# Gated delta rule: two heads to a step on a common beat, the inverse built from 32x32 blocks

## What is computed

```python
g = jnp.cumsum(g, axis=-1)                                  # per chunk
decay = jnp.exp(where(causal, g[c] - g[s], -inf))
lower = where(strict, (k_beta @ k.T) * decay, 0)
t_inv = inverse(eye + lower)                                # unit lower triangular
u = t_inv @ v_beta;  w = t_inv @ (k_beta * eg)
qk = where(causal, (q @ k.T) * decay, 0)
# over the chunks, state S:
v_new = u - w @ S;  o = q_g @ S + qk @ v_new;  S = S * exp(g_last) + k_dec.T @ v_new
o = rms_norm(o, gdn_norm_w) * silu(z)
```

## Time and profile before

| | us |
|---|---|
| median of 3 runs | 921.08 (913.3, 921.08, 924.0) |
| the profiled execution | 913.96 |
| its span, first to last instruction | 912.2 |
| PE busy in the span | 881.9 |
| DVE busy | 669.5 |
| ACT busy | 508.0 |
| POOL busy | 72.1 |

### The profile page before, as it was taken

One profiled execution on the slowest core, in us unless ns is written; L12 is line 12 of the kernel. 1 busy time (PEld: TensorE's weight loads), 2 busy tenths in 40 slices (PEclk: granted clock), 3 DMA queues, 4 the chain that ended last, 5 costly groups with the idle time before them and its releaser, 6 DMA issues.

```text
span 912.2 us, 18654 instructions
## 1 busy us (share of the span) xinstructions
PE 881.9 (97%) x8020; PEld 840.6 (92%) x8020; DVE 669.5 (73%) x1132; ACT 508.0 (56%) x822; POOL 72.1 (8%) x91
## 2 busy tenths in 40 slices
PE   5897999999999999999999999999999999999997
PEld 2797899999898989999999999999888999999997
DVE  3877877566979687677888885578666778888653
ACT  2489668453344637655354444556665567666442
POOL 0101122021001101020000000220000200000011
PEclk9999999999999999999999999999999999999999
DMA  8754232332776664465998889635332436555631
GB/s 337 277 190 170 93 137 97 139 139 97 248 259 230 233 231 164 167 216 182 269 338 292 286 291 259 227 121 189 137 141 93 182 139 210 207 185 175 251 130 47
DMA packets 27681, 177.31 MB, mean 194 GB/s; under 512 B 2864, under 2 KB 5680, under 8 KB 7504
## 3 DMA queue, kind: packets, MB, share of 16 engines
q1 hardware_dynamic: 27600, 176.13, 55.1%
HBM read 174.29 MB, written 1.84 MB: 193 GB/s over the span
## 4 chain that ended last, share of the span: by engine, by line
PE 76%; DVE 10%; ACT 7%; DMA 4%; issue 1%; POOL 1%; DVEq 0%; SPq 0%; ACTq 0%
PE ps L1094 42%; PE ps L1100 20%; DVE wl L1851 3%; DMA raw<-in_w_fi_dram 2%; ACT wh L1459 2%; DVE acc L1750 2%; PE ps L1092 2%; PE ps L1139 1%; PE ps L1147 1%; PE ps L1233 1%; PE ps L1150 1%; PE ps L1098 1%; DMA raw<-in_ada_dram 1%; DMA raw<-in_w_sc_dram 1%; DVE KT L1733 1%
## 5 line engine op out<-in xcount | busy, mean ns | idle before, releaser
L1851 DVE TENSOR_TENSOR wl<-raw,wh 128x1024 fp32r<-128x1024 f32 x265 | 322.0, 1235 | 76.2 <-ACT wh L1459 75.5
L1094 PE MATMUL ps<-HH,wh 128*128 128x256 f32 x1480 | 367.4, 285 | 0.7 <-ACT HH L1433 0.2
L1094 PE MATMUL ps<-HH,wl 128*128 128x256 f32 x1480 | 357.4, 278 | 0.0
L1459 ACT ACTIVATE wh<-raw 128x1024 fp32r<-128x1024 f32 x265 | 273.4, 1042 | 140.3 <-PE ps L1100 109.2
L1094 PEld LDWEIGHTS ps<-HH,wh 128*128 128x128 f32 x1480 | 279.2, 189 | 8.2 <-issue 2.9
L1094 PEld LDWEIGHTS ps<-HH,wl 128*128 128x128 f32 x1480 | 278.9, 188 | 0.4
L1100 PE MATMUL ps<-HL,wh 128*128 128x256 f32 x1480 | 226.6, 278 | 0.3 <-DVE HL L1796 0.3
L1100 PEld LDWEIGHTS ps<-HL,wh 128*128 128x128 f32 x1480 | 195.2, 188 | 0.6 <-DVE HL L1796 0.5
L1094 PE MATMUL ps<-FH,wh 128*128 128x256 f32 x352 | 84.5, 276 | 0.0
L1094 PE MATMUL ps<-FH,wl 128*128 128x256 f32 x352 | 84.5, 276 | 0.0
L1750 DVE SCALAR_TENSOR_TENSOR acc<-raw,silc,acc 128x512 f32<-128x512 f32 x101 | 76.3, 756 | 8.0 <-DMA raw<-in_ada_dram 5.0
(11 more groups left out here) (273 smaller groups left out, 1088.2 us busy)
## 6 DMA issues: line engine op xcount, KB each, us to landing
raw<-in_ada_dram SPq DMA_DIRECT2D x32, 1024.0 KB, 5.4
raw<-in_w_fi_dram SPq DMA_DIRECT2D x22, 1024.0 KB, 5.0
raw<-in_w_up_dram SPq DMA_DIRECT2D x22, 1024.0 KB, 4.8
raw<-in_w_rest_dram SPq DMA_DIRECT2D x20, 1024.0 KB, 4.7
raw<-in_w_in_dram SPq DMA_DIRECT2D x16, 1024.0 KB, 4.8
raw<-in_w_qkv_dram SPq DMA_DIRECT2D x12, 1024.0 KB, 4.8
raw<-in_w_o_dram SPq DMA_DIRECT2D x8, 1024.0 KB, 4.9
raw<-in_w_fo_dram SPq DMA_DIRECT2D x8, 1024.0 KB, 4.9
```

The costliest lines, as they stand in the source:

```text
L1094: e.matmul(o, w[:, k, 128 * t:128 * t + 128], x_hi[:, k0 + k, :], start=first and n + k == 0, **MM)
L1459: e.activation(whl[u % HALF][0][:, 0:n], raw[i % RAW][:, c:c + n], ACT.Copy).then_inc(*a_hi.up(u))
L1851: e.tensor_tensor(wl[:, 0:n], raw[i % RAW][:, c:c + n], wh[:, 0:n].bitcast(F32), ALU.subtract).then_inc(*v_lo.up(u))
```

## The change

One task now takes two heads (2j and 2j+1), so there are four tasks `gdn(j)` instead of eight; three streams stay, each with buffers for two heads, and buffers that are dead by then are laid under later ones (dec under inv, l2 and v under sh, qk under sl, d under s1 and k0, lc under y). The steps lie on even ticks, two ticks apart, with four ticks behind k = 0, 1, 10 and 19. K^T Q moves from k = 1 to the new k = 2. The inverse is doubled up to blocks of 32 only (LEVELS without 32), in 32x32 matmuls over the four quarters of the partitions. Only z is kept up to date by matmul; x is z turned by a 32x32 transpose on VectorE. Steps 11 and 12 join 32 to 64, steps 13 and 14 join 64 to 128. K is turned in step 15. GH and GL are filled up to 128 rows with zeros, so that k = 0 uses weights of 128 rows. The scaling of K (k0) moves from DVE to ACT, Q's decay (qg) from DVE to POOL, the masked d of all levels are made by one POOL instruction, and POOL places the blocks of z and x in inv and xy64 at k = 11.

```diff
-APART = 1
+GRID = 2
+HEAVY = (0, 1, 10, 19)
-LEVELS = [1, 2, 4, 8, 16, 32]
+LEVELS = [1, 2, 4, 8, 16]
...
     def beat(k):
+        for _ in range(2 if k in HEAVY else 1):
+            yield
+            while ticks[0] % GRID:
+                yield
...
-        tasks.append(gdn(2 * j))
-        tasks.append(gdn(2 * j + 1))
+        tasks.append(gdn(j))
...
+    def gdn(j):
+        while not open_streams:
+            yield
+        st, before_pair[j] = open_streams.pop(0)
+        while ("decays", 4, 0) not in made:
+            yield
+        yield from beat(2)
+        for k in range(21):
+            emit("gdn", j, k, st)
+            emit("gdn_out", j, k + 1, st)
+            if k < 20:
+                yield from beat(k)
+        open_streams.append((st, j))
...
+        if k == 0:
+            for i, h in heads_of:
+                one_hot = eyeR[:, h:h + 1].to_broadcast([128, 128])
+                e.matmul(bank[:, T * i:T * i + T], one_hot, GH[:, :], start=True, **MM)
+                ins = e.matmul(bank[:, T * i:T * i + T], one_hot, GL[:, :], start=False, **MM)
+        elif k == 1:
+            a_gdn.wait_ge(e, "eg", j)
+            for i, h in heads_of:
+                for c in range(2):
+                    ins = e.matmul(b4[:, 2 * i + c, :], KT[:, h, cs[c]], KT[:, h, cs[c]], start=True, **MM)
+        elif k == 2:
+            v_gdn.wait_ge(e, "l2", j, 3)
+            for i, h in heads_of:
+                for c in range(2):
+                    ins = e.matmul(b4[:, 2 * i + c, :], KT[:, h, cs[c]], QT[:, h, cs[c]], start=True, **MM)
+        elif k < 11 and k % 2:
+            n = (k - 1) // 2
+            if n == 1:
+                v_gdn.wait_ge(e, "qk", j)
+                g_gdn.wait_ge(e, "d", j)
+            v_gdn.wait_ge(e, "x", j, n - 1)
+            for i in range(4):
+                for q in quarter:
+                    ins = e.matmul(bank[q, 32 * i:32 * i + 32], S["d"][q, n - 1, i, :], x[q, i, :], start=True, **MM)
+        elif k < 11:
+            a_gdn.wait_ge(e, "y", j, n)
+            for i in range(4):
+                for q in quarter:
+                    ins = e.matmul(bank[q, 128 + 32 * i:160 + 32 * i], y[q, i, :], z[q, i, :], start=True, **MM)
+        elif k == 11:
+            for i in range(4):
+                for g in (0, 2):
+                    ins = e.matmul(bank[quarter[g + 1], 32 * i:32 * i + 32],
+                                   l2[quarter[g], i, 32 * g + 32:32 * g + 64], x[quarter[g], i, :], start=True, **MM)
+        elif k == 12:
+            for i in range(4):
+                for g in (0, 2):
+                    e.matmul(bank[quarter[g], 128 + 32 * i:160 + 32 * i], y[q, i, :], z[q, i, :], start=True, **MM)
+                ins = e.matmul(bank[quarter[1], 256 + 32 * i:288 + 32 * i], z[quarter[1], i, :], y[quarter[1], i, :],
+                               start=True, **MM)
+        elif k == 13:
+            for i in range(4):
+                ins = e.matmul(bank[hi, 64 * i:64 * i + 64], l2[lo, i, hi], S["xy64"][lo, i, :], start=True, **MM)
+        elif k == 14:
+            for i in range(4):
+                ins = e.matmul(bank[lo, 256 + 64 * i:320 + 64 * i], S["xy64"][hi, i, :], S["inv"][hi, i, hi], ...)
...
+        elif 5 <= k < 12 and k % 2:                       # VectorE
+            e.tensor_tensor(z[:, :, :], z[:, :, :], by_four(S, 128), ALU.subtract)
+            e.transpose(x, z)
...
+                if k == 2:                                # GpSimd
+                    e.tensor_tensor(S["d"][:, :, :, :], S["lc"][:, None, :, :].broadcast_to([128, 4, 4, 32]),
+                                    lev[:, 1:5, None, :].broadcast_to([128, 4, 4, 32]), ALU.mult)
+                    e.tensor_tensor(S["qg"][:, :, :], S["qg"][:, :, :], QT[:, 2 * j:2 * j + 2, c1], ALU.mult)
+                elif k == 11:
+                    for name, out, turned, blocks in (("x64", S["xy64"], S["x"], 2), ("inv", S["inv"], S["z"], 4)):
+                        e.tensor_tensor(out, turned, own, ALU.mult)
```

More of the change, by code:

```diff
@@ L36 @@
 _at = 0
-for _name, _n in (("eye", 128), ("ones", 128), ("eps", 1), ("lnq", 1), ("cmask", 128), ("eye64", 64), ("lev", 6 * 64)):
+for _name, _n in (("eye", 128), ("ones", 128), ("eps", 1), ("lnq", 1), ("cmask", 128), ("eye32", 32), ("own", 4), ("lev", 5 * 32)):
     CST[_name] = _at
@@ L248, in _program, with stream, one, early @@
     dt_y, dt_abs, dt_g = (M[0:8, n, :] for n in range(3))
[L249 to L258, removed]
+    def stream(i):
+        S = {}
+        def one(name, shape, dt=F32, where=mixer):
+            S[name] = sb(f"{name}{i}", shape, dt, where=where)
+        def early(name, shape):
+            with ExitStack() as turn:
+                one(name, shape, where=turn)
+        early("dec", [128, 4, 128])
+        one("inv", [128, 4, 128])
+        early("l2", [128, 4, 128])
+        early("v", [128, 2, 2, 128])
+        one("sh", [128, 512], F32R)
+        early("qk", [128, 4, 128])
+        one("sl", [128, 512], F32R)
+        early("d", [128, 4, 4, 32])
+        one("s1", [128, 2, 128])
+        one("k0", [128, 2, 128])
+        early("lc", [128, 4, 32])
+        one("y", [128, 4, 32])
+        one("z", [128, 4, 32])
+        one("x", [128, 4, 32])
+        one("xy64", [128, 4, 64])
+        one("qg", [128, 2, 128])
+        S["bank"] = psum[5 + i]
+        return S
+    streams = [stream(i) for i in range(STREAMS)]
     mixer.close()
@@ L1109, in pe_gdn @@
             a_misc.wait_ge(e, "onesR")
             v_misc.wait_ge(e, "GL")
[L1111 to L1114, removed]
-            v_misc.wait_ge(e, "l2", j, 1)
[L1116 to L1123, removed]
-        elif k == 2:
[L1125 to L1130, removed]
+            if before_pair[j] is not None:
+                a_gdn.wait_ge(e, "ln", before_pair[j])
@@ L1167, in pe_gdn @@
+            ins.then_inc(*p_gdn.up(j, k))
         elif k == 16:
-            v_gdn.wait_ge(e, "v0", h)
-            e.matmul(bank[:, c0], S["k0"][:, :], S["v"][:, 0, :], start=True, **MM).then_inc(*p_gdn.up(h, k))
+            a_gdn.wait_ge(e, "k0", j)
+            for i in range(2):
+                ins = e.matmul(bank[:, 128 * i:128 * i + 128], S["k0"][:, i, :], S["v"][:, i, 0, :], start=True, **MM)
+            ins.then_inc(*p_gdn.up(j, k))
         elif k == 17:
-            a_gdn.wait_ge(e, "s1", h)
```

397 lines of the change are left out of this document (211 added, 186 removed).

## The result

The changed kernel takes 888.64 us (median of 4 runs, 885.46 to 892.1), the kernel before 921.98 us on the same chip: 0.966 of it, 95% interval 0.958 to 0.973. In two more series, on other chips, the same pair stood at 0.964 (0.959 to 0.970) and 0.966 (0.964 to 0.968). The forecast was 886 us.

A forecast was written before the change was run, and what follows sets the result against it. TensorE (PE), busy 881.9 of 912.2 us, was taken as the bound through most of the delta rule. 19.6 + 11 + 5 - 4 = 31.6 us saved, from 918 to a median of 886 us; range 868 to 908, its own 874 to 898.

The forecast's parts named there:

- A: Small matmuls of the delta rule: 34.6 us before, 15 after, with 32x32 records at 0.008 us each; 19.6 us saved.
- B: Wide matmuls (K^T K, K^T Q, products with V, K, state and Q, 0.22 us each): same number, nothing saved.
- C: TensorE's trips to small tiles and back in the delta rule, 0.34 us each: 24 us becomes 13, 11 us saved.
- D: PE's waits in the delta rule, mostly before K^T K, and the slow clock behind: 10.1 to 5, 5 us saved.
- E: Added subtraction and transpose on VectorE at every level, behind convolutions and splits: late steps, 4 us lost.
- the 200 of the mark: Sign that the forecast is right: the last L1120 (K^T K) of the delta rule comes before 200 us.
- 1: Rival, small matmuls: 32 columns cost as much as 64, 0.015 to 0.02 us a record; 893 to 898 us; chance 0.17.
- 3: Rival, small matmuls: the quarters run in turn, 0.032 to 0.036 us a record; 911 to 915 us; chance 0.08.
- 4: Rival, steps 3 to 10: each 32x32 record takes a full 0.060 us, in turn; 939 us; chance 0.03.
- 2: Rival, q, k, v stretch: DVE becomes the bound, beats that meet a convolution 1 us late; 901 us; chance 0.11.
- 5: Rival, delta rule: pairs do not meet and steps wait for streams; costs 3 us, within the range; no chance given.

## Why the prediction held

**What bounds.** Right. PE set the time before and sets it after (in 200:360 it doesn't stand at all); of 32 us taken from its work in the delta rule all but the part below reached the end.

**A, the small matmuls (19.6 us).** Right in number and price. Steps 3 to 10 were put at 0.008 a record and 8.2 us; the group of 32 gives 0.25, 32 groups of them 8.0. A lone step 11 takes 0.37 and a lone step 12 0.38 us, steps 13 and 14 take 0.60 each; less the fixed 0.13 that is 0.24, 0.25, 0.47 and 0.47, so four pairs cost 8.0 + 4 x 1.43 = 13.7 where I had 15. Term A is 34.6 - 13.7 = 20.9, about 21. The choice that mattered was to read the halves as abreast from the earlier trace rows and to carry that over to quarters. By the Trainium skill (TensorEngine Tiling (Array Packing), Restrictions and Gotchas) row tiles can't use one PSUM bank at the same time; the trace disagrees, with 32 records to one bank in 0.25 us. By the Trainium skill (the same page, Instruction Overhead) a matmul of 32 columns should take what one of 60 does; for these f32 operands the trace disagrees there too: a record of 32 columns holds its quarter for 0.032 us, one of 64 held its half for 0.060.

**B.** Right: step 0 with 128 rows of weights makes no trip, and the wide ones cost 0.22 as before.

**C, the trips (11 us).** Right. I had written 71 before; by the line of each record it is 69. After it is 36, the number worked out from the ticks, and the price of the edges is unchanged. 33 x 0.34 = 11.2 us. The run on odd ticks shows 11 of the trips come back when the pairs don't meet; what one costs is read from the timeline, since waits moved in that run too.

**D, the waits (5 us saved).** This is the step of the working that failed. The prediction had "10.1 to 5" and, as its mark, "the longest wait of PE between 80 and 280 us under 2.5 us and PEclk near 1.00 there". The waits at K^T K did go, but the sum is 6.0 + 1.6 + 1.4 + some smaller ones, 9.6 us against 8.6; the longest is 4.0 as before, and the clock in 100:160 is 0.94, 3.6 us of full clock, against 1.8 in 80:100 before. That is 13.2 us against 10.1 before: D was a loss of some 3, not a gain of 5. I had looked only at the chain of the step itself (masks, exponentials) and not at what else the plan puts ahead of its copy on ScalarE, though the same block had been behind the 4.0 us of before.

**E, VectorE's longer chain (4 us lost).** The mechanism is there (1.6 us at qk behind splits and a convolution) but DVE is not late with x once in the changed kernel, so next to nothing was lost where I had 4 us (the 1.6 is counted in D). Its new transpose takes 0.31 us:

```profile
L1735 DVE STREAM_TRANSPOSE x<-z 128x128 f32<-128x128 f32 x16 | 5.0, 312 | 0.5
L1733 DVE TENSOR_TENSOR z<-z,ps 128x128 f32<-128x128 f32 x16 | 4.5, 280 | 7.4 <-PE ps L1171 7.1
```

DVE is busy for 47.06 of 60 us in 100:160, 78%, not the 85 to 90% I gave it, because PE's waits stretch the time: with ScalarE's block in three parts it is 50.88, 85%. GpSimd's large pieces (1.2 us for all d, 1.66 for inv) are hidden as said: no wait of PE from 80 to 290 us names them. The delta rule ends at 284 us, where 280 was said; K^T K of the last pair comes at 202, just past the 200 of the mark.

**The sum.** A 21, C 11.2, D and E together -3: 29 us. The profiled pair shows 22.2 us of span. What lies between is no part of the change: the pace of the split matmuls, below, took 6 to 7 us more in the profiled execution of the changed kernel than in that of before. The traces can be cut where that pace counts for little: for the delta rule in the profiles the kernel before takes 308.8 us and the changed one 279.1, 278.9 and 278.9 in its three profiles. So 29.8 us are saved there, as the terms say. The medians are 33 and 32 us apart in the first two series, and 31 in the last; the 1 to 3 us above 29.8 are not placed. Against 31.6, A is 1 better, D 8 worse and E 4 better. That D and E miss in opposite directions is luck, so the forecast was a little better than its working. One bound of the range was reckoned wrongly: with C at 17, D at 10 and E at 0 the low end is 871 from the 918 of the forecast; 868 follows only from 913.96.

**The rivals.** 1, 3 and 4 fell with the group of 0.38 us and the doubled matmuls. 2 (VectorE the bound) fell; the engine that was late is ScalarE. 5 fell with 36 trips.

## What to carry to other kernels

Where small matmuls stand between large ones, count first how often TensorE changes to small tiles and back (here 0.34 us each, more than what is done in them), put the steps of independent chains into the same gap, and order the small ones so that neighbours use different quarters of the rows. When work is written into one order for all engines, what decides a short step is what stands ahead of its copy on the slowest queue: look at the longest block there, not only at the step's own chain. Such waits move with each shift of the order (three parts of a block won 5 us; four, with one tick more, lost 7), so a change of it has to be timed, not reasoned.

## What the runs showed of the hardware

**Two paces of TensorE at one clock.** Split matmuls of 256 columns start either every 0.113 us or every 0.118 us, with PEclk 1.00 in both. The stretch from 740 to 860 us, whose code is the same in all, of the kernel before:

```profile
740.00:860.00 120.00, 120.00 (x1061) 120.00 (x1061) 100.07 (x152) 75.92 (x108) 0.00 (x0) 1.00 0.57 202
```

of the changed kernel's first profile:

```profile
740.00:860.00 120.00, 120.00 (x1022) 120.00 (x1021) 86.87 (x124) 67.06 (x91) 3.07 (x3) 1.00 0.55 193
```

and of its third:

```profile
740.00:860.00 120.00, 120.00 (x1062) 120.00 (x1061) 89.62 (x126) 69.06 (x93) 3.07 (x3) 1.00 0.53 193
```

1061 or 1022 starts in 120 us. A pace holds over the whole last third; in the delta rule it changes from group to group. Of 6264 split matmuls that each trace holds, about 1500 were at the slower pace before and 2850 in the first profile after, which at 0.0047 us apiece is 6.3 us. The time from the 2041st split matmul to the end says the same: 534.5 us before, 541.5 and 541.1 in the first two profiles of the changed kernel, 534.3 in the third. The same source showed the slower pace twice and the faster once. So between two profiled executions of one source the pace is worth 7 us, more than the 6.4 by which their spans differ (888.8 and 882.4). The executions profiled with the slower one were the slowest of their kernel (892.1 of 885.46 to 892.1; 890.58 of 882.12 to 890.58), the one with the faster in the middle of its series (884.18 of 881.69 to 885.97). Of the other versions the one on odd ticks and the one on three ticks show the slower pace (540.9 and 541.8 us for the last stretch), and both executions were the slowest of their series; all the rest show the faster (533.8 to 535.5). This would explain much of the spread between executions, but the pace is only seen in profiled ones, so that is argued and not shown. What sets it was not found, nor whether the change makes the slower one more frequent.

**Quarters side by side.** Four records of 32 columns in four quarters start 7, 7, 7 and 12 ns apart, about 32 ns for four, all into one PSUM bank; of one quarter, one starts every 32 ns. Up to 36 records in a row kept this rhythm in the doubled groups; behind them the starts come in twos, 2 and 15 ns apart, at nearly the same mean.
